# Merging two places of small work per unit into one in an encoder layer on one core

## The chip, the cores and the metric

One core of a Trainium2 chip runs the kernel. The metric is the device time of one execution in microseconds (us). TensorE (PE in the profile), VectorE (DVE), ScalarE (ACT), GpSimd (POOL) and SyncE (SP) each work through their own list in order and meet only through semaphores.

## The reference

One layer of a streaming encoder, for 512 prompt rows and 64 sample rows (576 columns once transposed), with 1024 features, in float32:

```python
h = rmsnorm(x, g_mix_pre)
q_a, k_a, v_a, q_r, k_r, v_r, g_r, gate_a, gate_r = split_in(h @ w_in)
o_a = attend(q_a, k_a, v_a, sinks)      # 8 heads, window of 128 rows, blocks of 64
o_r, ret_state = retain(rotary(q_r), rotary(k_r) * 128 ** -0.5, v_r)   # 4 heads, a state of 128 x 256
o_r = head_group_norm(o_r) * silu(g_r)
merged = sigmoid(gate_a) * (o_a @ w_branch_attn) + sigmoid(gate_r) * (o_r @ w_branch_ret)
x = x + rmsnorm(merged @ w_out, g_mix_post)
f = (silu(h2 @ w_ffn_gate) * (h2 @ w_ffn_up)) @ w_ffn_down     # h2 = rmsnorm(x, g_ffn_pre)
x = x + rmsnorm(f, g_ffn_post)
x = x + (p @ w_ple_proj) * sigmoid(x @ w_ple_gate)
```

## The kernel before

The big products are made of **units**. A unit is one 128-column tile of a weight against all 576 activation columns: 8 tiles of the contracted dimension, 3 products each (high and low parts of weight and activation), 2 halves of 288 columns, so 48 matmuls at line 683 into `acc`. Its weight is loaded by SyncE, copied to a high part by ScalarE (`split_hi`, L1140) and to a low part by VectorE (`split_lo`, L1630). When it is done VectorE takes it out of PSUM (`scaled_out`, L1660, called by `job_out` in the heads). There are two accumulators and two weight slots.

Between the matmuls of these units TensorE does the attention and the retention in small **pieces**. The layer has five rounds of six units. In round `h` = 0 to 3 the units are the projections of retention head `h` (first unit to sixth, `t` = 0 to 5); a last round is the first six of the gate units. Beside them round `h` does attention block `h` (block 4 in the last), and the retention of head `h - 1`, which takes five chunks `c`. Round 0 has no retention. Rounds 1 to 3 are one loop.

`PLACES` is a list of twelve lists of pieces, written out by hand; all engines walk the same list. The pieces are:

- `("att", "A", p)`: TensorE scores (L829), VectorE scale, mask and maximum (L1737), ScalarE exponentials (L1203).
- `("att", "N", p)`: VectorE alone: denominator, reciprocal, and four scalings of `prob` (L1749, L1751, L1754).
- `("att", "B", p)`: TensorE transposes `prob` (L838); VectorE (L1759) and ScalarE (L1209) copy them to `prob_t`. In block 0 there is only VectorE's copy.
- `("att", "C", p)`: TensorE multiplies with v (L846), ScalarE copies the result to `o_att` (L1216).
- `("ret", "A", c)`: TensorE L860 and L863, VectorE q_dec, s_dec, k_dec. `("ret", "B", c)`: TensorE L875, L877, L879; VectorE updates the state and takes the moments; GpSimd the power. `("ret", "N", c)`: VectorE norms (L1793). `("ret", "C", c)`: TensorE transposes `o_norm` (L887), VectorE multiplies with the gate (L1801).
- `("v", None, e)`: TensorE transposes half of v (L898, L899), VectorE copies it out (L1831, L1833).

TensorE, in `six_jobs`, does the even place `2t` after 24 of the 48 matmuls of unit `t`, and the odd place `2t + 1` behind its last matmul. On VectorE `head` (and the gate loop) does for each `t`: place `2t`, `job_out(t)`, place `2t + 1`, the low part of unit `t + 2`'s weight, and the rotation in `t` = 0 and 2. ScalarE does place `2t`, the high part of unit `t + 2`, its own work on unit `t` (swaps, sigmoids), place `2t + 1`. GpSimd: place `2t`, its own work, place `2t + 1`.

Waits that matter below are those on TensorE: `B` of attention waits for `att_prob` (the last scaling of `N`); `C` of attention for `att_t0` and `att_t1` (the two copies); `ret C` for `ret_norm`; `ret A` of chunk `c` for `ret_gated` of chunk `c - 2` and before; `v` for `att_out` (ScalarE's copy after `C`). On VectorE `ret C` waits for TensorE's `ret C` (`ret_C`). A place's pieces stand in order on every engine, so on VectorE place 7, `[("ret", "C", 2), ("att", "N", 1)]`, does the gate product of chunk 2 and then the scalings.

Of the kernel before, what the change touches and what calls it, by code (L numbers as in the profile page):

```python
# [14 lines left out]
P = 128  # L15
# [6 lines left out]
KD = D // P  # L22
HEADS, KV, HD = 8, 2, 64
GROUP = HEADS // KV
# [26 lines left out]
U_GATE, J_GATE = U_HEAD + 6 * RH, J_HEAD + 6 * RH  # L51
U_MRG, J_MRG = U_GATE + 8, J_GATE + 8
# [50 lines left out]
def unit(base, step=0, i=0):  # L103

    return base // 2 + (step // 2) * i, base % 2
# [6 lines left out]
def wait(eng, sem, value):  # L112

    if not (isinstance(value, int) and value <= 0):
        eng.wait_ge(sem, value)
# [4 lines left out]
    [("att", "N", 0)],  # L120
    [("ret", "B", 0), ("ret", "A", 1), ("ret", "N", 0)],
    [("att", "B", 0), ("ret", "C", 0)],
    [("att", "C", 0), ("ret", "B", 1), ("ret", "A", 2), ("ret", "N", 1)],
    [("ret", "C", 1), ("att", "A", 1)],
    [("ret", "B", 2), ("ret", "A", 3), ("ret", "N", 2)],
    [("ret", "C", 2), ("att", "N", 1)],
# [166 lines left out]
def encoder_layer(nc, x_p, x_s, p_p, p_s, cache_k, cache_v, state_in, g_mix_pre, w_in, sinks_in,  # L293
                  w_ba, w_br, w_out, g_mix_post, g_ffn_pre, w_fg, w_fu, w_fd, g_ffn_post, w_pp, w_pg,
                  table_in, scratch, y_p, y_s, k_p, v_p, r_p, k_s, v_s, r_s):
    with ExitStack() as ctx:
# [3 lines left out]
        def place(name, shape, dt=F32, at=None):  # L300

            size = int(np.prod(shape[1:])) * 4
            if at is None:
                at = cursor[0]
                cursor[0] += (size + 31) // 32 * 32
            assert at + size <= nc.sbuf_usable_end, (name, at + size, nc.sbuf_usable_end)
            return nc.alloc_sbuf_tensor_at(name, shape, dt, offset=at)
# [35 lines left out]
        xh = place("xh", [P, KD, ROWS], F32R, at=a_at)  # L343
        xl = place("xl", [P, KD, ROWS], F32R, at=b_at)
# [103 lines left out]
        att = small[:, 0:1024]  # L448
# [72 lines left out]
        def acc_of(a):  # L521
            return acc[:, a, :, 0:HALF]
# [37 lines left out]
        def halves(ap):  # L560
            return ap.rearrange("p (h n) -> p h n", h=2)
# [113 lines left out]
        def _(pe):  # L675
            def products(s, a, ks, rhs_h, rhs_l, first, last, tile_at):

                ins = None
                for n, k in enumerate(ks):
                    at = tile_at(k)  # L680
                    for m, (w, x) in enumerate(((whi, rhs_h), (whi, rhs_l), (wlo, rhs_h))):
                        for hf in range(2):
                            ins = nc.tensor.matmul(  # L683
                                acc[:, a, hf, 0:HALF], w[:, s, at:at + P], x(k)[:, hf * HALF:(hf + 1) * HALF],
                                start=first and n == 0 and m == 0, stop=last and n == len(ks) - 1 and m == 2)
                return ins

            def run_unit(vs, wa, rhs, ks=KD, k0=0, first=True, last=True, ready=None,
                         between=None):


                (v, s), (w, a) = vs, wa
                if first:
                    wait(pe, acc_free[a], w)
                pe.wait_ge(lo_ready, 2 * v + s + 1)
                rh_, rl_ = rhs
                if between is not None:
                    for part in (range(ks // 2), range(ks // 2, ks)):
                        ins = products(s, a, part, lambda k: rh_[:, k, :], lambda k: rl_[:, k, :],
                                       part[0] == 0, part[-1] == ks - 1, lambda k: k * P)  # L700
                        if part[0] == 0:
                            between()
                elif ready is None:
                    ins = products(s, a, range(ks), lambda k: rh_[:, k0 + k, :], lambda k: rl_[:, k0 + k, :],
                                   first, last, lambda k: k * P)
                else:
                    for k in range(ks):
                        ready(k0 + k)
                        ins = products(s, a, [k], lambda k: rh_[:, k0 + k, :], lambda k: rl_[:, k0 + k, :],
                                       first and k == 0, last and k == ks - 1, lambda k: k * P)  # L710
                ins.then_inc(unit_done, 1)
# [178 lines left out]
            def v_transposes(e, h):  # L890

                w, a = unit(J_HEAD + (3, 4)[e], 6, h)
                pe.wait_ge(acc_free[a], w + 1)
                wait(pe, v_rows, 2 * h + e)
                pe.wait_ge(att_t1, 2 * h + 2)
                pe.wait_ge(att_out, 2 * h + 2)
                for r in range(RT - 1):
                    nc.tensor.transpose(att[:, r * P:(r + 1) * P], zt[:, a, r * P:(r + 1) * P], ident)  # L898
                nc.tensor.transpose(att[0:DEC, SEQ:SEQ + P], zt[:, a, SEQ:ROWS], ident).then_inc(v_t, 1)  # L899

            def pieces(place, h, b, r, slot):
                for kind, piece, c in PLACES[place]:
                    if kind == "att":
                        att_piece(piece, c, b)
                    elif kind == "ret" and r is not None:
                        ret_piece(piece, c, r, slot)
                    elif kind == "v" and h is not None:
                        v_transposes(c, h)

            def six_jobs(u, j, per, i, h, b, r, slot):  # L910

                for t in range(6):
                    run_unit(unit(u + t, per, i), unit(j + t, per, i), (xh, xl),
                             between=lambda: pieces(2 * t, h, b, r, slot))
                    pieces(2 * t + 1, h, b, r, slot)

            pe.wait_ge(ckt_ready, 1)
            pe.wait_ge(kv_rows, 1)
# [702 lines left out]
        def _(dve):  # L1621
# [4 lines left out]
            def split_lo(vs, n=KD * P):  # L1626

                v, s = vs
                dve.wait_ge(hi_ready, 2 * v + s + 1)
                nc.vector.tensor_tensor(wlo[:, s, 0:n], raw[:, s, 0:n], whi[:, s, 0:n].bitcast(F32),  # L1630
                                        ALU.subtract).then_inc(lo_ready, 1)
# [25 lines left out]
            def scaled_out(dst, w, a, u):  # L1657

                dve.wait_ge(unit_done, u + 1)
                nc.vector.tensor_tensor(halves(dst), acc_of(a), halves(rb[:, :]), ALU.mult).then_inc(acc_free[a], 1)  # L1660
# [150 lines left out]
            def rotate(t, h, slot):  # L1811

                m = 2 * h + t // 2
                dve.wait_ge(swap_ready, m + 1)
                nc.vector.tensor_tensor(tb[:, :], tb[:, :], rot[:, 1, :], ALU.mult).then_inc(dve_rot, 1)
                dve.wait_ge(dve_rot, m + 1)
                dve.wait_ge(cos_ready, m + 1)
                if not isinstance(h, int):

                    dve.wait_ge(ret_A, 5 * (h - 1) + CREDIT)  # L1820
                    dve.wait_ge(ret_kst, 5 * (h - 1) + CREDIT)
                dst = (qr if t == 0 else kr)[:, span(slot, 1), 0:ROWS].rearrange("p a n -> p (a n)")
                nc.vector.tensor_tensor(dst, ta[:, :], tb[:, :], ALU.add).then_inc(rotated, 1)
# [12 lines left out]
            def pieces(place, h, b, r, slot, rslot):  # L1836
                for kind, piece, c in PLACES[place]:
                    if kind == "att":
                        att_piece(piece, c, b)
                    elif kind == "ret" and r is not None:  # L1840
                        ret_piece(piece, c, r, rslot)
                    elif kind == "v" and h is not None:
                        v_out(c, h, slot)

            def head(h, b, r, slot, rslot):
                for t in range(6):
                    pieces(2 * t, h, b, r, slot, rslot)
                    job_out(t, h)
                    pieces(2 * t + 1, h, b, r, slot, rslot)
                    split_lo(unit(U_HEAD + t + 2, 6, h))  # L1850
                    if t in (0, 2):
                        rotate(t, h, slot)

            head(0, 0, None, 0, None)
            with dve.Fori(1, RH) as h:
                head(h, h, h - 1, h % 2, (h - 1) % 2)
# [9 lines left out]
            for t in range(8):  # L1866
                if t < 6:
                    pieces(2 * t, None, RH, RH - 1, None, (RH - 1) % 2)
                w, a = unit(J_GATE + t)
                if t == 1:  # L1870
                    dve.wait_ge(g_ready, 2 * RH)
                wait(dve, gate_sig[a], t // 2)
                scaled_out(zt[:, a, :], w, a, U_GATE + t)
                if t < 6:
                    pieces(2 * t + 1, None, RH, RH - 1, None, (RH - 1) % 2)
                split_lo(unit(U_GATE + t + 2) if t < 6 else unit(U_MRG + t - 6), n=(GROUP if t == 6 else KD) * P)
                if t >= 5:
                    branch_parts(range(BRANCH_TILES[t - 5], BRANCH_TILES[t - 4]))
            def gated(u, j, per, c, n, slot, col):
# [427 lines left out]
            for n, e in enumerate(Y_ORDER):  # L2307
                _, c, h = e
# [191 lines left out]
```

## Time and profile before

| | |
|---|---|
| three runs | 986.4, 986.9, 987.0 us; median 986.9 |
| the profiled execution | 986.12 us, span 984.5 us, mean granted clock 0.999 |
| TensorE matmuls busy | 974.8 us (99% of the span) |
| VectorE, ScalarE, GpSimd busy | 634.1, 397.0, 86.5 us |
| the five rounds | from 61.7 to 319.5 us of the span |

In the profile's time tables each line is a group of instructions by source line. A matmul's listed duration runs from its start to its modelled end, and neighbours overlap, so the time that TensorE spends on something is read from one start to the next.

### The profile page before, as it was taken

What the parts mean: (1) busy time and instruction counts of PE and PEld (TensorE: products, weight loads), DVE (VectorE), ACT (ScalarE), POOL (GpSimd) and SP (SyncE); (2) the same over time, 40 slices, a digit from 0 to 9 for tenths busy, and PEclk for the clock granted to TensorE, in tenths of its full rate; (3) what the DMA queues carried; (4) which work ended last, traced back from release to release, by engine and by line L of the source; (5) the groups of instructions that cost most, each with busy time, mean ns of one, the idle gap of its engine ahead of it and who ended that gap; (6) DMA issues with size and microseconds to landing.
All of it is one profiled execution on the core that took longest, in us unless ns stands there. A gap on an engine that the chain in (4) does not pass through costs nothing.

```text
span 984.5 us, 19215 instructions
## 1 busy us (share of the span) xinstructions
PE 974.8 (99%) x7286; PEld 954.2 (97%) x7286; DVE 634.1 (64%) x1246; ACT 397.0 (40%) x695; POOL 86.5 (9%) x140
## 2 busy tenths in 40 slices
PE   9999999999999999999999999999999999999998
PEld 7999999999999999999999999999999999999997
DVE  6554676767665633445467899625996469966772
ACT  4333533434243522223555555424453234444352
POOL 2123212212100000010002000000000000030000
PEclk9999999999999999999999999999999999999999
DMA  8434222122222232245603523521334213366211
GB/s 214 137 123 121 79 66 72 46 75 62 62 70 65 76 94 78 78 129 180 179 12 122 190 79 94 150 66 44 101 108 127 73 50 107 97 202 189 86 48 50
DMA packets 166199, 98.47 MB, mean 100 GB/s; under 512 B 14657, under 2 KB 162529, under 8 KB 165873
## 3 DMA queue, kind: packets, MB, share of 16 engines
q1 hardware_dynamic: 159904, 79.19, 28.4%
q0 software_dynamic: 4336, 16.67, 4.7%
q10 hardware_dynamic: 1888, 1.64, 0.6%
q8 instruction: 48, 0.79, 0.3%
q14 instruction: 23, 0.18, 0.1%
HBM read 86.79 MB, written 10.75 MB: 99 GB/s over the span
## 4 chain that ended last, share of the span: by engine, by line
PE 91%; DVE 5%; issue 2%; ACT 1%; DMA 0%; DVEq 0%; SPq 0%; ACTq 0%
PE acc L683 34%; PE acc L960 10%; PE acc L961 10%; PE acc L962 10%; PE small L960 6%; PE small L961 6%; PE small L962 6%; PE small L829 1%; PE small L846 1%; PE small L875 1%; PE small L879 1%; PE small L877 1%; PE acc L791 1%; PE small L1114 1%; ACT prob L1203 1%
## 5 line engine op out<-in xcount | busy, mean ns | idle before, releaser
L683 PE MATMUL acc<-xh,whi 128*128 128x288 f32 x720 | 159.0, 302 | 0.7 <-DVE xl L1653 0.7
L683 PE MATMUL acc<-xl,whi 128*128 128x288 f32 x720 | 153.3, 294 | 0.0
L683 PE MATMUL acc<-xh,wlo 128*128 128x288 f32 x720 | 153.3, 294 | 0.0
L1140 ACT ACTIVATE whi<-raw 128x1024 fp32r<-128x1024 f32 (+1 forms) x61 | 61.1, 1002 | 203.7 <-PE acc L683 201.5
L683 PEld LDWEIGHTS acc<-xh,whi 128*128 128x128 f32 x720 | 113.9, 188 | 5.0 <-issue 3.4
L683 PEld LDWEIGHTS acc<-xl,whi 128*128 128x128 f32 x720 | 115.0, 188 | 0.0
L683 PEld LDWEIGHTS acc<-xh,wlo 128*128 128x128 f32 x720 | 114.9, 188 | 0.0
L1954 DVE TENSOR_TENSOR wlo<-raw,whi 128x512 fp32r<-128x512 f32 (+2 forms) x93 | 81.0, 872 | 49.9 <-ACT whi L1354 34.2
L960 PE MATMUL acc<-yh,whi 128*128 128x288 f32 x360 | 107.2, 298 | 0.6 <-DVE yl L2014 0.5
L962 PE MATMUL acc<-yh,wlo 128*128 128x288 f32 x360 | 106.1, 295 | 0.0
L1630 DVE TENSOR_TENSOR wlo<-raw,whi 128x1024 fp32r<-128x1024 f32 (+1 forms) x63 | 73.0, 1159 | 43.6 <-ACT whi L1140 43.0
L960 PE MATMUL acc<-fh,whi 128*128 128x288 f32 x264 | 77.9, 295 | 0.0
L961 PE MATMUL acc<-fl,whi 128*128 128x288 f32 x264 | 77.8, 295 | 0.0
L962 PE MATMUL acc<-fh,wlo 128*128 128x288 f32 x264 | 77.7, 294 | 0.0
L961 PE MATMUL acc<-yl,whi 128*128 128x288 f32 x264 | 77.7, 294 | 0.0
L1362 ACT ACTIVATE whi<-s_sum 128x512 fp32r<-128x512 f32 x76 | 47.7, 630 | 61.5 <-DVE s_sum L2135 50.0
L960 PEld LDWEIGHTS acc<-yh,whi 128*128 128x128 f32 x360 | 67.6, 188 | 1.1 <-DVE yl L2014 1.1
L962 PEld LDWEIGHTS acc<-yh,wlo 128*128 128x128 f32 x360 | 67.6, 188 | 0.0
L1660 DVE TENSOR_TENSOR zt<-acc,rb 128x576 f32<-128x576 f32 x40 | 30.3, 756 | 45.8 <-PE acc L683 45.8
L1954 DVE TENSOR_TENSOR wlo<-s_sum,whi 128x512 fp32r<-128x512 f32 x76 | 51.7, 684 | 8.6 <-ACT whi L1362 8.6
L1354 ACT ACTIVATE whi<-raw 128x1024 fp32r<-128x1024 f32 (+1 forms) x38 | 38.2, 1011 | 39.9 <-PE acc L962 18.1
L961 PEld LDWEIGHTS acc<-yl,whi 128*128 128x128 f32 x264 | 49.6, 188 | 0.0
(326 smaller groups left out, 2398.0 us busy)
## 6 DMA issues: line engine op xcount, KB each, us to landing
raw<-in_w_in SPq DMA_DIRECT2D x92, 256.0 KB, 3.2
raw<-in_w_ffn_gate SPq DMA_DIRECT2D x44, 256.0 KB, 3.2
raw<-in_w_ffn_up SPq DMA_DIRECT2D x44, 256.0 KB, 4.1
raw<-in_w_ffn_down SPq DMA_DIRECT2D x32, 256.0 KB, 3.6
res<-x_scratch POOLq DMA_DIRECT2D x16, 288.0 KB, 4.2
raw<-in_w_branch_ret SPq DMA_DIRECT2D x16, 256.0 KB, 3.0
raw<-in_w_out SPq DMA_DIRECT2D x16, 256.0 KB, 4.9
raw<-in_w_ffn_down SPq DMA_DIRECT2D x16, 192.0 KB, 3.7
```

The source lines that it names most:

```text
L683: ins = nc.tensor.matmul(acc[:, a, hf, 0:HALF], w[:, s, at:at + P], x(k)[:, hf * HALF:(hf + 1) * HALF], start=first and n == 0 and m == 0, ...
L791: ins = nc.tensor.matmul(acc[:, 0, hf, 0:HALF], w[:, at], x[:, k, hf * HALF:(hf + 1) * HALF], start=k == 0 and m == 0, stop=k == KD - 1 an ...
L829: ins = nc.tensor.matmul(att[0:nq, slot * KW + k0:slot * KW + k1], q_st[64 * g:64 * g + 64, 2 * p + j, 0:nq], k_st[64 * g:64 * g + 64, k0: ...
L960: nc.tensor.matmul(bank, w_h, x_h, start=first, stop=False)
L961: nc.tensor.matmul(bank, w_h, x_l, start=False, stop=False)
L962: return nc.tensor.matmul(bank, w_l, x_h, start=False, stop=last)
L1140: nc.scalar.activation(whi[:, s, 0:n], raw[:, s, 0:n], ACT.Copy).then_inc(hi_ready, 1)
L1354: nc.scalar.activation(dst[:, 0:n], raw_of(RAW[u])[:, 0:n], ACT.Copy).then_inc(hi_ready, 1)
L1362: nc.scalar.activation(dst[:, 0:QUART], s_sum[:, S_STEP[u[2]], :], ACT.Copy).then_inc(hi_ready, 1)
L1630: nc.vector.tensor_tensor(wlo[:, s, 0:n], raw[:, s, 0:n], whi[:, s, 0:n].bitcast(F32), ALU.subtract).then_inc(lo_ready, 1)
L1660: nc.vector.tensor_tensor(halves(dst), acc_of(a), halves(rb[:, :]), ALU.mult).then_inc(acc_free[a], 1)
L1954: nc.vector.tensor_tensor(dst[:, 0:n], src[:, 0:n], high[:, 0:n], ALU.subtract).then_inc(lo_ready, 1)
```

## The change

Two edits of order on TensorE, one on VectorE, and one list reordered. TensorE does both the odd place `2t - 1` and the even place `2t` in the middle of unit `t`, one right behind the other; place 11 stays behind unit 5. On VectorE the odd place is moved behind the low part and the rotation. Place 4 is reordered so that `("att", "C", 0)` is its last piece. ScalarE and GpSimd keep their order, except for place 4, where each of them has at most one of its kinds in the same order as before.

```diff
@@ PLACES
     [("att", "B", 0), ("ret", "C", 0)],
-    [("att", "C", 0), ("ret", "B", 1), ("ret", "A", 2), ("ret", "N", 1)],
+    [("ret", "B", 1), ("ret", "A", 2), ("ret", "N", 1), ("att", "C", 0)],
     [("ret", "C", 1), ("att", "A", 1)],
@@ TensorE, six_jobs
+                def inside(t):
+                    if t > 0:
+                        pieces(2 * t - 1, h, b, r, slot)
+                    pieces(2 * t, h, b, r, slot)
+
                 for t in range(6):
-                    run_unit(unit(u + t, per, i), unit(j + t, per, i), (xh, xl),
-                             between=lambda: pieces(2 * t, h, b, r, slot))
-                    pieces(2 * t + 1, h, b, r, slot)
+                    run_unit(unit(u + t, per, i), unit(j + t, per, i), (xh, xl), between=lambda: inside(t))
+                pieces(11, h, b, r, slot)
@@ VectorE, head
                     job_out(t, h)
-                    pieces(2 * t + 1, h, b, r, slot, rslot)
                     split_lo(unit(U_HEAD + t + 2, 6, h))
                     if t in (0, 2):
                         rotate(t, h, slot)
+                    pieces(2 * t + 1, h, b, r, slot, rslot)
@@ VectorE, gate units
                 scaled_out(zt[:, a, :], w, a, U_GATE + t)
+                split_lo(unit(U_GATE + t + 2) if t < 6 else unit(U_MRG + t - 6), n=(GROUP if t == 6 else KD) * P)
                 if t < 6:
                     pieces(2 * t + 1, None, RH, RH - 1, None, (RH - 1) % 2)
-                split_lo(unit(U_GATE + t + 2) if t < 6 else unit(U_MRG + t - 6), n=(GROUP if t == 6 else KD) * P)
```

## Rows read from the trace of the kernel before

**Rows 1.** The page: busy us, share of the span and instructions of each engine.
```profile
PE 974.8 (99%) x7286; PEld 954.2 (97%) x7286; DVE 634.1 (64%) x1246; ACT 397.0 (40%) x695; POOL 86.5 (9%) x140
```

**Rows 2.** Stretches: round 2, last round (length, busy us by engine, clock, DMA).
```profile
160.16:215.28 55.12, 54.94 (x401) 51.41 (x401) 38.36 (x99) 21.66 (x39) 11.07 (x18) 1.00 0.22 64
...
270.35:319.45 49.10, 49.10 (x368) 46.03 (x368) 29.43 (x89) 18.18 (x37) 4.58 (x10) 1.00 0.23 68
```

**Rows 3.** Waits of TensorE, 60 to 330 us: total us, times, longest.
```profile
PE small L887 <- DVE o_norm L1793: 0.6, 3, 0.2
```

**Rows 4.** Timeline of TensorE, round 2, end of unit 3, middle of 4: start, us.
```profile
192.50 0.38 PE L887 MATMUL small<-tab,o_norm 128*128 128x128 f32 x2
192.63 0.51 PE L683 MATMUL acc<-xh,whi 128*128 128x288 f32 x2
192.98 0.42 PE L683 MATMUL acc<-xl,whi 128*128 128x288 f32 x2
...
195.89 1.03 PE L838 MATMUL small<-tab,prob 128*128 128x128 f32 x8
196.76 0.60 PE L875 MATMUL small<-vr,s_dec 128*128 x2
```

**Rows 5.** The chain of waits in order of time, round 2: start, us, what.
```profile
178.21 0.63 PE small L875 x2
...
192.88 3.17 PE acc L683 x24
...
196.92 0.43 PE small L875 x2
...
202.96 3.37 PE acc L683 x24
```

**Rows 6.** Timeline of TensorE and VectorE, round 2, end of unit 1.
```profile
172.30 1.03 PE L838 MATMUL small<-tab,prob 128*128 128x128 f32 x8
173.52 0.44 PE L887 MATMUL small<-tab,o_norm 128*128 128x128 f32 x2 [0.18 <-DVE o_norm L1793]
...
172.91 0.54 DVE L1793 TENSOR_SCALAR o_norm<-small,moments,grstd 128x256 f32<-128x256 f32 x1
```

**Rows 7.** Timeline of VectorE, round 2, place 7 and the copy of place 8.
```profile
193.37 0.41 DVE L1801 TENSOR_TENSOR o_ret<-small,gr 128x256 f32 x1
193.70 0.15 DVE L1749 TENSOR_TENSOR den<-den,sink_exp 128x4 f32<-128x4 f32 x1
...
194.10 1.14 DVE L1754 TENSOR_SCALAR prob<-prob,den 128x256 f32<-128x256 f32 x4
...
196.96 0.69 DVE L1759 COPY prob_t<-small 128x512 f32<-128x512 f32 x1 [0.58 <-PE small L838]
```

**Rows 8.** Timeline of VectorE, last round, place 7.
```profile
302.23 0.41 DVE L1801 TENSOR_TENSOR o_ret<-small,gr 128x256 f32<-128x256 f32 x1
...
302.95 1.00 DVE L1754 TENSOR_SCALAR prob<-prob,den 64x192 f32<-64x192 f32 x4
```

**Rows 9.** Timeline of ScalarE, VectorE and TensorE, round 0, units 3 and 4.
```profile
86.94 1.06 ACT L1140 ACTIVATE whi<-raw 128x1024 fp32r<-128x1024 f32 x1 [1.65 <-PE acc L683]
...
88.02 0.88 DVE L1754 TENSOR_SCALAR prob<-prob,den 128x128 f32<-128x128 f32 x4
88.81 1.22 DVE L1630 TENSOR_TENSOR wlo<-raw,whi 128x1024 fp32r<-128x1024 f32 x1
90.49 0.69 DVE L1759 COPY prob_t<-small 128x512 f32<-128x512 f32 x1 [0.46 <-PE small L838]
...
89.85 0.60 PE L838 MATMUL small<-tab,prob 128*128 128x128 f32 x4
```

**Rows 10.** Timeline of TensorE and ScalarE, round 2: attention C and its copy.
```profile
201.88 1.08 PE L846 MATMUL small<-prob_t,v_st 128*64 128x256 f32 x8
...
203.17 0.39 ACT L1216 ACTIVATE o_att<-small 128x256 f32 x1 [0.35 <-PE small L846]
```

**Rows 11.** Stretch at the end of the span: last column but two is the clock.
```profile
982.00:984.50 2.50, 0.00 (x0) 0.00 (x0) 0.00 (x0) 0.00 (x0) 0.00 (x0) 0.61 0.23 59
```

## The prediction

> **What bounds the kernel now.** I read the page first: TensorE is busy 974.8 of 984.5 us, the next engine 634.1 [rows 1]. So a change of order can save only what TensorE waits or loses at a switch, and a new wait on TensorE is paid in full, because no idle time behind it can take it up. Then the stretches: round 2 takes 55.12 us and the last round 49.10, with the clock at 1.00 and VectorE busy 38.36 of 55.12 [rows 2]. Rounds 1 and 3 repeat round 2 within 0.05 us. Then TensorE's waits: in all five rounds there is one kind, `ret C` for `o_norm`, three times [rows 3]. The timelines give the sizes of the rest.
>
> **What a stop of the unit's stream costs.** The change moves 19 groups of pieces on TensorE from a unit's end to a middle: places 3, 5, 7 and 9 in four rounds, and 3, 5 and 9 in round 0, where place 7 has nothing for TensorE (nor has place 1 anywhere). 18 of them join a stop that exists already. In steady stream 24 matmuls take 3.17 us, 0.264 a pair [rows 5]. At the end of unit 3 `ret C` starts at 192.50 and the next unit's first pair at 192.63; that pair takes 0.35 instead of 0.264, so the stop takes 0.13 + 0.09 = 0.22 us. Eight transposes take 196.76 - 195.89 = 0.87, 0.109 each, so the two of `ret C` are 0.22 by themselves [rows 4]. A stop costs nothing beyond its own work, and merging stops gains 0 to 0.02 each; I take 0. The pieces on half the rows (attention A and C) lose about 0.2 us behind them, into the main stream (3.37 against 3.17) as into another piece (0.63 against 0.43 for the same pair) [rows 5]. Place 4's reordering therefore exchanges one such loss for an equal one: 0, at most 0.1 a round either way.
>
> **What is saved.** At the end of unit 1 the transposes of attention B start at 172.30 and need 0.87, but `ret C` starts at 173.52, behind `o_norm`, which VectorE ends at 173.45 [rows 6]. 173.52 - 173.17 = 0.35 us, and 0.3 to 0.4 in rounds 1 and 3 (three waits [rows 3]): 1.1 us. With the change `ret C 0` comes 3.2 us later and this wait goes. VectorE's low parts now stand earlier, but TensorE waits for none of them today, so that is worth 0.
>
> **What is added.** The same rule for each: two pieces that were half a unit (3.2 us of TensorE's own work) apart are now neighbours, and where another engine has a step between them TensorE stands.
>
> *Place 7 to place 8, rounds 1 to 3.* TensorE does `ret C 2`, then attention B 1, which needs the scalings of N 1. VectorE has N 1 behind its own `ret C 2`, and that waits for TensorE's `ret C 2`, now in the middle of unit 4. So the whole VectorE chain starts only then. From a transposition's listed end to VectorE's start takes 0.04 us (195.89 + 1.03 = 196.92, start 196.96) [rows 4, 7]; `ret C` is listed at 0.38 [rows 4], so VectorE starts at +0.42. From its `ret C` to the end of the last scaling it is 194.10 + 1.14 - 193.37 = 1.87 [rows 7], and back to TensorE 0.07 (173.45 to 173.52 [rows 6]): +2.36. Without the wait TensorE would go on at +0.22. **2.14 us a round, 6.4 in three.** Behind the waiting VectorE instruction stand only the copy of B 1 and `ret B 3`, for which TensorE isn't yet ready.
>
> *The same in the last round.* 302.95 + 1.00 - 302.23 = 1.72 [rows 8] in place of 1.87: **2.0 us.**
>
> *Round 0.* It has no `ret C`, but N 1 moves behind the low part of unit 5, whose high part ScalarE ends at 88.00 [rows 9]. Low part 1.15 (its 1.22 less the overlap with its successor), 0.40 to the scalings [rows 7], 0.88 for them [rows 9] and 0.1 of hand-over: 90.53, where B 1 starts at 89.85 today [rows 9]. **0.7 us.** Also, with no retention between them B 0 and C 0 are now neighbours: B starts, VectorE's copy starts 0.64 later (90.49 against 89.85) and takes 0.69 [rows 9], +1.39 with the hand-over, against 0.54 for four transposes and the switch: **0.85 us.** And C 1 and `v 0`: ScalarE starts 0.21 after C's listed end (201.88 + 1.08 to 203.17) and takes 0.39 [rows 10]; C of block 0 has half the passes, some 0.65 listed, so +1.3 against 0.55: **0.75 us.**
>
> *What is covered.* In rounds 1 to 4 `ret B 1` and `ret A 2` (1.3 + 0.33) stand between B 0 and C 0. VectorE's copy and `ret C 0` are done at 1.07 + 0.6 + 0.4 = 2.1 us after B's start, `ret A 2` comes at 0.87 + 0.22 + 1.3 = 2.4, C 0 at 2.8. `ret B 4` (1.3) stands between C 1 and `v 0`, and ScalarE needs 0.7. For place 5 `ret C 1`, VectorE comes from the rotation some 0.9 us late, but `ret A 3`, which wants its result, comes 2.7 us later. Bounds: 0 if the covers hold, 0.3 to 0.5 a piece in four rounds if one is short, 2 us. I take 0. VectorE's bunched work (3 to 5 us behind each middle) fits the 3.2 us of the second half and the pieces before it, with 0.2 to 0.8 us left in units 3 and 5; what is late first is `job_out`, which has a whole unit of slack. The branch parts behind the last round start about a low part (1.2 us [rows 9]) later, and their first reader comes two units (4 x 3.17 us) behind.
>
> **The sum.** 6.4 + 2.0 + 0.7 + 0.85 + 0.75 - 1.1 = 9.6 us. On the profiled execution: 986.1 + 9.6 = 995.7 us. The median of the runs is 0.8 above it, which gives 996.5; between them **996**. Bounds of the terms: each chain of place 7 can be 0.3 shorter or 0.2 longer, round 0's three together 1.0 to 2.8: 994 to 998.5.
>
> **The clock, against the trace.** The granted clock is 1.00 in every round, and the one stretch below it is the last 2.5 us, 0.61, when TensorE had run dry [rows 11]; the change adds four holes of 2 us in the middle of a unit. The Trainium skill ("TensorE: Matmul & The Clock Gate", section "HAM oscillation — how this bites in real kernels") says that waits between bursts of matmuls can throttle the array and that every burst after them then starts cold. If each of the four holes cost the 3.17 us half behind it at 1.2 GHz, twice as long, it would be 4 x 3.2 = 13 us on top. The end of the span agrees in direction; no row shows a 2 us hole inside a busy stretch.
>
> **Rivals.**
> *A. The stops are what costs, and the time falls.* Were the switch between float32 pieces and the stream expensive, 19 groups merged would each return it. For it: a round's 55.12 less twelve halves of 3.17 leaves 17.1, of which the passes explain 15.1, so 1.9 is lost at borders. Against: 4 x 0.3 to 0.4 of that stands at the half-row pieces, which keep their borders, and 0.35 is `o_norm`. It decides from (9.6 / 19) 0.5 us a stop; at 0.55 each: 986.1 + 9.6 - 10.5 = 985.2 us.
> *B. The chain of place 7 is mostly covered.* If VectorE could take N 1 ahead (TensorE and the exponentials were early enough) only round 0 and a hand-over of 0.5 us a round stay: 2.3 + 2 - 1.1 = 3.2, 989.5 us. Against: one list, one order, and VectorE executes in order.
> *C. A cover is short.* VectorE's bunched work makes TensorE wait at C 0, `ret A` or `v` too, 1 to 1.5 us a round in four rounds: 5 on top, 1001.
> *D. The clock falls* behind the new holes: 1009.
>
> **How the numbers follow.** Forecast 72%, C 10%, B 9%, A 5%, D 4%. The range from 991 to 1001 leaves out A, B's lower half, D and half of C; the forecast's own is 994 to 998.5. No change can be told within 0.2% (2 us). Slower by more: forecast, C, D and B (3.2 us, its lower part within 2): 0.92. Same: 0.04; faster: 0.04, both from A.
>
> **What would show it.** Round 2 at 55.1 + 2.14 - 0.35 = 56.9 us, the last at 51.1, and round 0 longer by 2.3. A new row in TensorE's waits, L838 for VectorE's `prob` (L1754), five times and about 2 us in four of them; no `ret C` wait for `o_norm`; in round 0 waits of L846 for `prob_t` and of L898 for `o_att`. After the rounds nothing changes: the stretch from the rounds' end to the span's end stays at 665 us. Wrong would be: no L838 wait, halves shorter than 3.17, a clock below 1.00 in the rounds, or waits for the low part at L683.

## The result: 1003.4 us, slower by 1.6%

| | before | after |
|---|---|---|
| median of 5 runs each | 986.7 us | 1003.4 us (1000.1 to 1003.6) |
| ratio | 1 | 1.0163 (95%: 1.0150 to 1.0175) |
| profiled execution: span, granted clock | 984.5 us, 0.999 | 1001.7 us, 0.995 |
| round 0, from first to next attention A | 43.30 us | 46.34 us |
| rounds 1, 2, 3 | 55.13, 55.12, 55.07 | 59.19, 59.03, 57.31 |
| last round, to the first unbroken unit behind it | 49.10 | 52.62 |
| from there to the end of the span | 665.05 | 665.08 |

The direction was forecast, the size was not: 996 us with a range to 1001. The five rounds together are 16.8 us longer, the rest is equal within 0.1, but for 0.4 us while the input loads. That part ahead of the rounds takes 61.7 to 63.7 us in the profiled executions of this document, though no edit touches it; so a difference of 1 to 2 us between two medians says less than the stretches of the rounds. The stretches of the changed kernel, columns as in [rows 2]:

```profile
108.47:167.66 59.19, 56.82 (x402) 52.53 (x401) 39.37 (x99) 22.04 (x39) 11.76 (x19) 0.97 0.22 66
167.66:226.69 59.03, 56.89 (x402) 52.62 (x401) 39.26 (x99) 21.83 (x39) 11.02 (x18) 0.97 0.21 60
226.69:284.00 57.31, 55.16 (x402) 51.22 (x403) 39.26 (x99) 21.84 (x41) 11.01 (x18) 1.00 0.21 62
```

The third column from the end answers to the 1.00 of [rows 2]: it is 0.97 in rounds 1 and 2 and 1.00 in round 3. Where it is 1.00 the round is 1.7 to 1.9 us shorter. TensorE's waits, which before had one kind in the rounds [rows 3]:

```profile
PE small L838 <- DVE prob L1758: 9.4, 5, 2.1
...
PE small L846 <- DVE prob_t L1763: 0.9, 1, 0.9
PE small L898 <- ACT o_att L1220: 0.7, 1, 0.7
```

These are the three handovers of the prediction, and `o_norm` is gone. Their sum is 11.0 us and the rounds grew by 16.8. The timeline of TensorE in round 2, the middle of unit 4 (before: [rows 4]), shows what the list of waits doesn't:

```profile
203.04 0.38 PE L887 MATMUL small<-tab,o_norm 128*128 128x128 f32 x2
205.56 1.78 PE L838 MATMUL small<-tab,prob 128*128 128x128 f32 x8 [2.13 <-DVE prob L1758]
207.13 1.06 PE L875 MATMUL small<-vr,s_dec 128*128 x2
207.99 1.06 PE L877 MATMUL small<-state_p,q_dec 128*128 128x256 f32 x2
208.84 0.78 PE L879 MATMUL small<-vr,k_dec 128*128 x2
209.46 0.38 PE L860 MATMUL small<-qr,rk_st 128*128 x2
```

From 203.04 to 205.56 there is 0.22 us of work and 2.30 of idle. Then eight transposes take 1.57 us (205.56 to 207.13) where they took 0.87 in [rows 4], and L875, L877 and L879 take 0.86, 0.85 and 0.62 in place of 0.43 each, until with L860 the normal pace is back. Together 1.7 us. From B 1 to attention C 1 it takes 10.90 us here (205.56 to 216.46) and 9.22 in round 3; I call such a stretch at the low clock a **dip**, and the idle time before it a **hole**. The same place in round 3, where nothing is slow:

```profile
262.02 0.38 PE L887 MATMUL small<-tab,o_norm 128*128 128x128 f32 x2
264.54 1.09 PE L838 MATMUL small<-tab,prob 128*128 128x128 f32 x8 [2.14 <-DVE prob L1758]
265.47 0.60 PE L875 MATMUL small<-vr,s_dec 128*128 x2
```

The stretches behind the holes of rounds 2, 1 and 3, and of the last round:

```profile
205.56:209.50 3.94, 3.94 (x15) 3.50 (x16) 0.69 (x1) 0.60 (x1) 0.00 (x0) 0.57 0.04 12
146.56:150.50 3.94, 3.94 (x18) 3.45 (x19) 1.17 (x3) 0.60 (x1) 0.00 (x0) 0.65 0.03 9
264.50:268.50 4.00, 3.96 (x28) 3.81 (x29) 2.03 (x7) 0.60 (x1) 0.10 (x1) 1.00 0.05 16
320.30:324.30 4.00, 3.98 (x21) 3.57 (x22) 1.50 (x6) 0.39 (x1) 0.00 (x0) 0.69 0.14 42
```

The granted clock is 0.57, 0.65, 1.00 and 0.69 there. So in three of the four retention rounds the clock fell from 2.4 to 1.2 GHz behind an idle hole, for the larger part of these stretches, and in round 3 it did not behind an equal hole. It did not fall in the hole itself: when TensorE had begun again, the clock was still at 2.4 GHz for 1.21 us in round 1, 0.24 in round 2 and 1.53 in the last. Executions of the one kernel differ: four of the five runs took 1003.3 to 1003.6 us at clock 0.994 or 0.995, the fifth 1000.1 us at 0.997, so it seems to have had fewer dips (only one run has a trace).

| the 16.8 us by part | forecast | measured in the profiled rounds |
|---|---|---|
| idle at place 7 to 8, rounds 1 to 3 and last | 6.4 + 2.0 | 3 x 2.30 + 1.98 = 8.9 |
| the same in round 0 (N 1 behind the low part) | 0.7 | 92.58 - 91.20 = 1.4 |
| round 0, B 0 to C 0 and C 1 to v 0 | 0.85 + 0.75 | 0.94 + 0.76 = 1.7 |
| slow passes behind three holes (B 1 to C 1, with the dip less without) | 0 | 10.87 and 10.90 less 9.22, last round 10.61 less 9.01 (experiments 1 and 2): 4.9 |
| wait for o_norm gone | -1.1 | -1.1 |
| rest, 0.5 in round 1, 0.3 in rounds 2 and 3 (retention A 2 late by 0.4 and 0.17, borders) | 0 | 1.0 |
| sum | 9.6 | 16.8 |

### The profile page after: what moved, and what is told of

Its sections match the earlier page's. It is cut to its first block, busy times and chain, and to the rows that moved or that the text cites. A ratio compares the mean times of both kernels' runs of the same rounds, so it can differ in the third digit from the quotient of the medians.

```text
span 1001.7 us, 19215 instructions
## 1 busy us (share of the span) xinstructions
PE 980.1 (98%) x7286; PEld 957.1 (96%) x7286; DVE 638.8 (64%) x1246; ACT 398.0 (40%) x695; POOL 85.4 (9%) x140
## 4 chain that ended last, share of the span: by engine, by line
PE 92%; DVE 4%; issue 1%; ACT 1%; DMA 1%; SPq 0%; DVEq 0%; ACTq 0%
PE acc L683 35%; PE acc L964 10%; PE acc L966 10%; PE acc L965 10%; PE small L964 6%; PE small L965 6%; PE small L966 6%; PE small L875 1%; PE small L879 1%; PE small L838 1%; PE small L846 1%; PE small L829 1%; PE small L877 1%; PE acc L791 1%; PE small L860 1%
## 5 line engine op out<-in xcount | busy, mean ns | idle before, releaser
L1634 DVE TENSOR_TENSOR wlo<-raw,whi 128x1024 fp32r<-128x1024 f32 (+1 forms) x63 | 79.3, 1259 | 55.4 <-ACT whi L1144 54.9
```

## The experiments

"Before" below is the kernel before, run on the same chip in the same turns (three groups of runs, each on a chip of its own); its medians were 986.5 to 986.9 us.

**1. Place 7 turned round.** All engines do N 1 ahead of C 2:

```diff
-    [("ret", "C", 2), ("att", "N", 1)],
+    [("att", "N", 1), ("ret", "C", 2)],
```

> The changed kernel with place 7 turned round: attention N 1 ahead of retention C 2, on every engine. VectorE can then scale prob before TensorE reaches C 2. Theory (a hole of 2.3 us in each of four rounds, and behind three of them a stretch at 1.2 GHz that costs 1.75 us): both go, 4 x 2.3 + 3 x 1.75 = 14.4 us less than 1003.4, so 989 us, granted clock 1.00 in all rounds, round 0 still 3.0 us longer than before the change. Rival (bunching the small work is itself what costs, VectorE is late all over): the time falls by less than half of that, to 996 or more. Rival (the clock falls for the new order of pieces, not for the hole): 994, with the clock still 0.97 in three rounds.

Measured 992.8 us, 1.0059 of before (1.0045 to 1.0073). Both the holes of 2.3 us and the slow passes are gone, 10.6 us. The theory wanted 14.4; a smaller hole is left. TensorE in round 2:

```profile
200.69 0.38 PE L887 MATMUL small<-tab,o_norm 128*128 128x128 f32 x2
201.61 1.09 PE L838 MATMUL small<-tab,prob 128*128 128x128 f32 x8 [0.54 <-DVE prob L1758]
```

201.61 - 200.69 - 0.22 = 0.70 us idle: VectorE does N 1 behind the low part of unit 5 (1.14 us, and 0.22 of waiting for ScalarE's high part before it), and it comes to it late, behind a low part of unit 4 that took 2.25 us in place of 1.22 (more on that behind experiment 10). No slow passes follow. Neither rival fits: the clock is 1.00 in all rounds.

**2. The hole filled with useless matmuls.**

```diff
+                    if t == 4 and r is not None:
+                        for _ in range(10):
+                            nc.tensor.matmul(ret_dl[:, 0:P], ones[:, :], ones[:, :], start=True, stop=True)
```

> The changed kernel with ten float32 matmuls of ones by ones (128x128x128, about 2.2 us at full clock) between places 7 and 8 in the rounds with retention; their result is used by nothing. TensorE now works in the hole but is not earlier at attention B 1. Theory (the idle hole makes the granted clock fall): the hole's 2.3 us stay, the slow passes behind it go: 1003.4 - 5.2 = 998 us, clock 1.00 in the rounds. Rival (the passes behind the hole are slow because of the bunched pieces or of contention on PSUM, and the clock column only reports it): still 1003 to 1004, attention B's eight transposes still 1.6 us.

Measured 999.6 us, 1.0126 (1.0111 to 1.0142); 998 was expected. TensorE in round 2, and the stretch of that round:

```profile
202.49 0.38 PE L887 MATMUL small<-tab,o_norm 128*128 128x128 f32 x2
202.70 2.40 PE L917 MATMUL small<-ones 128*128 128x128 f32 x20
205.00 1.09 PE L838 MATMUL small<-tab,prob 128*128 128x128 f32 x8
205.93 0.60 PE L875 MATMUL small<-vr,s_dec 128*128 x2
```

```profile
167.13:224.46 57.33, 57.32 (x421) 53.50 (x421) 39.24 (x99) 21.82 (x39) 11.00 (x18) 1.00 0.21 62
```

Attention B starts as late as with the hole (2.3 us behind C 2), and its eight transposes take 0.93 again. 57.33 us is round 3 of the changed kernel (57.31), which had the hole and no dip. So the hole's own length and the slow passes are two costs, and the second hangs on TensorE being idle. The five rounds take 270.0 us, 4.5 less than in the changed kernel. Useless work made the kernel faster. (The profiled execution has one low clock some 12 us into the span, ahead of the rounds; the rounds have none.)

**3. Retention in the hole.**

```diff
-    [("att", "B", 1), ("ret", "B", 3), ("ret", "A", 4), ("ret", "N", 3)],
+    [("ret", "B", 3), ("ret", "A", 4), ("ret", "N", 3), ("att", "B", 1)],
```

> The changed kernel with place 8 reordered: retention B 3, A 4, N 3 ahead of attention B 1 (as the change itself did in place 4). Retention B 3 and A 4 take 1.3 + 0.33 us of TensorE and need only VectorE's gate product, so they fill 1.6 us of the 2.3 us hole. Theory: a hole of 0.65 us stays, too short to move the clock: 1003.4 - 4 x 1.6 - 5.2 = 992 us, clock 1.00. Rival (any stop for VectorE in the middle drops the clock): 997, clock still 0.97 in three rounds. Rival (bunching costs): over 997.

Measured 993.0 us, 1.0057 (1.0043 to 1.0071), as expected within 1. Round 2:

```profile
201.15 0.60 PE L875 MATMUL small<-vr,s_dec 128*128 x2
...
202.70 0.27 PE L863 MATMUL small<-tab,rk_st 128*128 128x128 f32 x1
203.45 1.09 PE L838 MATMUL small<-tab,prob 128*128 128x128 f32 x8 [0.48 <-DVE prob L1758]
```

From 202.81 to 203.45, 0.64 us, TensorE is idle, and no pass behind is slow: the clock is 1.00 in all rounds.

**4. VectorE's order back**, the odd place ahead of the low part and the rotation, here and in the same way in the gate units; TensorE as changed:

```diff
                     job_out(t, h)
+                    pieces(2 * t + 1, h, b, r, slot, rslot)
                     split_lo(unit(U_HEAD + t + 2, 6, h))
                     if t in (0, 2):
                         rotate(t, h, slot)
-                    pieces(2 * t + 1, h, b, r, slot, rslot)
```

> The changed kernel with VectorE's order as before the change (the odd place ahead of the low part and the rotation), TensorE and place 4 as changed. Theory (round 0's longest new wait, 1.4 us at attention B 1, comes from N 1 standing behind the low part): round 0 gets 1.4 us shorter, the four holes at place 7 stay as they are, since there VectorE waits for TensorE's retention C 2 in either order: 1002 us. The low parts then come after the holes, some 3.6 us before they are needed, so they add nothing. Rival (the low parts' place decides, and late ones stop the stream): waits of L683 for the low part, 1006 or more.

Measured 1001.9 us, 1.0142 (1.0124 to 1.0160): as expected. The wait of L838 in round 0 is gone (8.2 us in four, where it was 9.4 in five), the four of 2 us are there. One of its five runs took 997.6 us at clock 0.999, the others 1001.6 to 1002.4 at 0.992 to 0.995. The profiled one (1001.9) has three dips, and 1001.9 less three dips of 1.6 to 1.7 us is 997: it looks like the same kernel with and without them.

**5. One edit to the kernel before: retention C 0 later.**

```diff
-    [("att", "B", 0), ("ret", "C", 0)],
-    [("att", "C", 0), ("ret", "B", 1), ("ret", "A", 2), ("ret", "N", 1)],
+    [("att", "B", 0)],
+    [("ret", "C", 0), ("att", "C", 0), ("ret", "B", 1), ("ret", "A", 2), ("ret", "N", 1)],
```

> The kernel before the change, with one edit: retention C 0 moved from the end of unit 1 (place 3) to the head of place 4 in the middle of unit 2. Theory: this takes the wait for o_norm (0.35 us in three rounds) and nothing else; 986.9 - 1.1 = 985.8 us, no L887 wait left. Rival (the wait only moves, VectorE being late from round to round): 986.9 as before.

Measured 985.6 us, 0.9988 (0.9979 to 0.9997): the only kernel here that beats the one before, by 0.1%. The view of TensorE's waits has no row left in the rounds. Round 2 (55.12 before [rows 2]):

```profile
160.29:214.94 54.65, 54.65 (x401) 51.39 (x401) 38.45 (x99) 21.67 (x39) 10.98 (x18) 1.00 0.22 65
```

**6. Place 7 turned round and VectorE's order back** (edits 1 and 4).

> The changed kernel with place 7 turned round and VectorE's odd places ahead of the low parts again; TensorE still does both places in the middle. In the run with place 7 alone turned round, TensorE still stood 0.7 us before attention B 1 in each round and 1.4 in round 0. Theory (that rest is N 1 standing behind the low part, which waits for ScalarE's high part): it goes, 992.8 - 4 x 0.7 - 1.4 = 988.6 us. What is left over before the change is round 0's B-C and C-v waits (1.5 us) and 0.2 us a round at retention A 2, less the 1.1 saved. Rival (VectorE is simply late there, with its bunched work): 992 to 993.

Measured 993.5 us, 1.0064 (1.0050 to 1.0078): a miss, the theory's 988.6 is out. Round 0's wait went (44.9 us against 46.3) and so did the hole of the last round, but the hole of rounds 1 to 3 grew from 0.70 to 1.48. VectorE in round 2:

```profile
191.59 0.42 DVE L1805 TENSOR_TENSOR o_ret<-small,gr 128x256 f32 x1 [2.80 <-PE small L887]
...
194.72 1.23 DVE L1634 TENSOR_TENSOR wlo<-raw,whi 128x1024 fp32r<-128x1024 f32 x1
195.86 0.75 DVE L1819 TENSOR_TENSOR tb<-tb,rot 128x576 f32<-128x576 f32 x1
...
199.90 0.75 DVE L1664 TENSOR_TENSOR zt<-acc,rb 128x576 f32<-128x576 f32 x1
...
200.97 1.14 DVE L1758 TENSOR_SCALAR prob<-prob,den 128x256 f32<-128x256 f32 x4
```

VectorE idles 2.80 us for TensorE's C 1, and then has attention A 1, the low part, the rotation and retention B 2, A 3 and N 2 in one piece up to 200. The unit's result waits for it (0.75 at 199.90), and N 1 behind that ends at 202.1, where TensorE wanted it at 200.7. So the rival's reason is right here (its 992 to 993 is just missed): with this order VectorE is late. Between experiments 1 and 6 the change's order of VectorE is thus worth 0.5 to 0.7 us in each of rounds 1 to 3 and costs 1.4 in round 0 and 0.4 in the last: nearly nothing in sum. The three holes of 1.5 us brought no dip: clock 1.00 in the rounds.

**7. Round 0 apart**: the kernel of 6 with TensorE's round 0 as before the change (`if r is None` the old loop of `six_jobs`).

> The kernel of z1 with round 0's places apart on TensorE as before the change (the odd place at the unit's end); rounds 1 to 4 merged. Theory (in round 0 no retention stands between B 0 and C 0 or between C 1 and v 0, so merging costs 0.76 + 0.7 us there): 1.5 us less than z1, 987.1 us, equal to the kernel before within 0.5 us, so merging as such neither gains nor costs. Rival (merging stops saves switching, 0.05 us or more a stop): 985.9 or less. Rival (bunching costs): 988.5 or more.

Measured 991.0 us, 1.0044 (1.0031 to 1.0058). The step of 2.5 us from 6 is larger than the 1.5 expected; in the profiled executions round 0 gives 1.6 (43.30 us, exactly before's, against 44.89), and the part ahead of the rounds is 1.3 shorter, where nothing was changed. The level is off for the same reason as in 6.

**8. Place 4 in its old order** (attention C 0 first, otherwise as changed).

> The changed kernel with place 4 in its old order, attention C 0 first. Theory (C 0 then follows B 0 with only retention C 0 between, and VectorE's copy ends 1.83 us after B's start where TensorE comes at 1.09): a wait of 0.75 us at L846 in each of rounds 1 to 4, and retention A 2's 0.2 us wait goes: 1003.4 + 4 x 0.55 = 1005.6 us; should the clock fall for more of the holes, up to 1.75 us on top. Rival (the reordering is what brought the slow passes): 1000 or less.

Measured 1004.5 us, 1.0172 (1.0156 to 1.0188). The expected 1005.6 is missed by 1.1. The waits are there, 0.66 us in each of rounds 1 to 3 and 0.24 in the last (3.1 in all, with round 0's 0.9), where 0.75 was expected in four:

```profile
PE small L846 <- DVE prob_t L1763: 3.1, 5, 0.9
```

In the profiled execution the clock fell in two rounds instead of three, which hides part of it; round 3, with no dip in either, is 57.76 against 57.31. The reordering of place 4 is worth some 0.45 us in each of rounds 1 to 3 to the changed kernel.

**9. The chain alone in the kernel before.** Nothing merged, VectorE's order as before:

```diff
-    [("ret", "C", 2), ("att", "N", 1)],
-    [("att", "B", 1), ("ret", "B", 3), ("ret", "A", 4), ("ret", "N", 3)],
+    [],
+    [("ret", "C", 2), ("att", "N", 1), ("att", "B", 1), ("ret", "B", 3), ("ret", "A", 4), ("ret", "N", 3)],
```

> The kernel before the change, with one edit of PLACES: place 7 emptied and its two pieces put ahead of attention B 1 in place 8, so that retention C 2, N 1 and B 1 follow each other in the middle of unit 4 as in the changed kernel. No place is merged, VectorE's order is as before. Theory: this handover alone makes the idle stretch of 2.3 us in rounds 1 to 3 and 2.1 in the last, 0.7 us in round 0, and up to four dips of the clock behind them at 1.75 us: 986.9 + 9.0 + 0.7 + 3.5 to 7 = 1000 to 1003.6 us, with slow passes behind attention B 1. Rival (it needs the merged places or VectorE's changed order as well): 992 or less.

Measured 999.1 us, 1.0131 (1.0116 to 1.0147), 0.9 below the expected band. One handover makes 12.6 of the change's 16.7 us; in the profiled rounds it is 11.2 of 16.8. Round 2 and the last:

```profile
164.41:221.83 57.42, 55.10 (x401) 51.37 (x401) 38.52 (x99) 21.71 (x39) 11.11 (x18) 1.00 0.21 62
...
279.25:331.82 52.57, 50.76 (x368) 47.55 (x368) 29.58 (x89) 18.23 (x37) 4.59 (x10) 0.97 0.22 63
```

Rounds 1 to 3 are longer by 2.3 each with the clock at 1.00, the last by 3.5 with it at 0.97: here one hole of four brought a dip. The runs go from 998.4 us (clock 0.997) to 1000.9 (0.994).

**10. Merged and covered**: edits 1, 3 and 7, VectorE's order as changed.

> The changed kernel with all three remedies: place 7 turned round (N 1 first), place 8 with retention B 3 and A 4 ahead of attention B 1, round 0 apart on TensorE; VectorE's order as changed. Theory (only handovers without cover cost): rounds 1 to 4 like before the change less 0.35 for o_norm in three, plus 0.2 each at retention A 2; round 0 keeps 0.7 us at B 1 with N 1 behind the low part: 986.9 - 1.1 + 0.8 + 0.7 = 987.3 us, clock 1.00. Rival (merging stops pays once covered): 985.5 or less. Rival (VectorE bunched is late anyway): 990 or more.

Measured 988.8 us, 1.0021 (1.0012 to 1.0030), where 987.3 was expected; neither rival. Rounds 1 to 3 take 55.51, 55.22 and 55.19 us, the last 49.12, no more than 0.4 over before's; round 0 keeps 1.45 at attention B 1 instead of 0.7. Together that is 2.1 us. The only waits in the rounds:

```profile
PE small L838 <- DVE prob L1764: 1.2, 1, 1.2
...
PE small L860 <- issue: 0.3, 1, 0.3
```

**A side effect that the traces of all the kernels show.** In the change's order VectorE does the low part of unit 4's weight right behind the result of unit 2, and so beside GpSimd's multiplication `ta`, which starts with the same result; the low part of unit 2 stands behind unit 0 in the same way. Round 0 of the changed kernel, and the same low part before:

```profile
82.20 2.19 DVE L1634 TENSOR_TENSOR wlo<-raw,whi 128x1024 fp32r<-128x1024 f32 x1 [0.40 <-ACT whi L1144]
...
81.89 1.42 POOL L2398 TENSOR_TENSOR ta<-zt,rot 128x576 f32<-128x576 f32 x1 [4.13 <-DVE zt L1664]
```

```profile
82.10 1.22 DVE L1630 TENSOR_TENSOR wlo<-raw,whi 128x1024 fp32r<-128x1024 f32 x1
```

Each of the six kernels with the change's order of VectorE has eight such low parts, of units 2 and 4 in rounds 0 to 3: 1.66 to 1.68 us where 0.6 us of them lie beside `ta`, 2.08 to 2.26 where 1.0 to 1.2 do. The six with the old order (experiments 4 to 7 and 9, and the kernel before) have none beside `ta`, and one of 1.57 us in experiments 4 and 6, 0.5 us of it beside another such multiplication (`gr`). A low part at 533.38 us of the changed kernel, wholly beside GpSimd's power of 96 x 3 elements, takes 1.22.

## Why the prediction was wrong

**What bounds the kernel, and that waits on TensorE are paid in full:** right. Behind the rounds the two traces agree within 0.1 us.

**A stop costs nothing by itself:** right. 16 stops fewer in experiment 10 made no round shorter, though the 0.35 us of `o_norm` is gone in three; experiment 5 gets that gain with no merging. A gain of a few hundredths a stop could hide behind retention A 2's delay, but not rival A's 0.5.

**Place 7 to 8:** the place, the mechanism and the count are right, and 2.30 stands for 2.14. The missing 0.16 is VectorE's start, 0.58 us behind `ret C`'s start (203.04 to 203.62) where I had taken 0.42 from a wait behind other transposes; the chain itself took 1.88 against 1.87.

**"The clock falls", rival D at 4%:** this is the step that failed. The sum priced a hole at its length alone, and gave the clock only the form of all or nothing (13 us on top). In three of four rounds the clock fell, and each fall cost 1.6 to 1.7 us: 4.9 of the 7.2 us that the forecast was short. Experiment 2 shows it: the same delay with TensorE busy, and the passes are fast. Experiments 3, 4 and 9 agree. The page of the Trainium skill that the prediction cited ("TensorE: Matmul & The Clock Gate", section "HAM oscillation — how this bites in real kernels") warned rightly that waits between bursts can throttle. That every burst behind them starts cold the traces do not bear out: round 3 stayed at 2.4 GHz, and in the others the clock fell only when TensorE had begun again. The measured price was less than half of what I had built on it, since the clock did not fall behind every hole, and where it did, it was low for less work than the half unit that I had taken: in round 2 for the small pieces, in round 1 and the last for some of these and the first matmuls of the half unit. I had weighed it by the trace of before, in which [rows 11] shows the low clock only when TensorE had run dry, and that trace has no idle of this size inside the rounds; it could not speak against the rule.

**Round 0, N 1:** 1.4 instead of 0.7 us. I had let ScalarE begin unit 5's high part at the unit's end, as in [rows 9]. In the changed kernel it began 0.7 us behind the unit's end (88.3), after the exponentials of A 1:

```profile
82.20 2.19 DVE L1634 TENSOR_TENSOR wlo<-raw,whi 128x1024 fp32r<-128x1024 f32 x1 [0.40 <-ACT whi L1144]
84.31 0.75 DVE L1819 TENSOR_TENSOR tb<-tb,rot 128x576 f32<-128x576 f32 x1
...
88.93 0.19 ACT L1209 ACTIVATE sink_exp<-top 128x4 f32<-128x4 f32 x1
89.03 1.04 ACT L1144 ACTIVATE whi<-raw 128x1024 fp32r<-128x1024 f32 x1
```

Attention A 1 came half a unit later and the low part ahead of it on VectorE took 2.19 us instead of 1.22, beside GpSimd's `ta` (81.89 to 83.31). At 1.22 the exponentials would have ended before the unit did, an estimate from these rows. So a queue that I had called ready was not, because its work comes from the pieces that had moved. That the 1.4 us is N 1 behind the low part is shown by experiment 4. In all twelve traces a low part takes 1.5 us or more only beside a GpSimd multiplication; no run took the multiplication away.

**The covers:** they held at C 0 and at `v 0` of the later rounds. At `ret A 2` I had 0.3 us in hand, but it starts 0.17 late (185.54 against 185.37) in rounds 2 and 3, and 0.4 late in round 1, where VectorE's product also waited for GpSimd's `gr`:

```profile
184.67 0.42 DVE L1805 TENSOR_TENSOR o_ret<-small,gr 128x256 f32 x1
...
185.54 0.48 PE L860 MATMUL small<-qr,rk_st 128*128 x2
```

VectorE's product ends 2.1 us behind B's start (182.98 to 185.09), as estimated. What I had wrong is the way back: TensorE starts 0.45 behind it, in round 1 too, and not 0.07 as at `ret C`; why is open. With the half-row borders this is the 0.3 to 0.5 us a round that I had priced at 0.

**VectorE's room:** with the change's own order it fitted, as said. With the old order it does not once place 7 is turned round (experiment 6), which I had not expected.

**Open:** what decides whether a hole of 2.0 to 2.3 us brings a dip. Of the sixteen such holes in the profiled executions nine did: three of four in the changed kernel and in experiment 4, two in experiment 8, one in experiment 9; and runs of one kernel differ. Holes of 1.5 us and less (experiments 1, 3, 6, 7 and 10, and round 0 everywhere) brought none.

## What to carry to other kernels

When two groups of small work are moved together, list for each engine what the second needs from the first: a pair that passes through another engine needs that engine's whole chain as idle time, and order inside the merged list (independent work between, the other engine's long step first) decides more than the number of stops. Price an idle hole of TensorE at its length and a possible dip of the clock behind it; if it can't be closed, useless matmuls in it were better than none here. And follow a moved piece into the queues that it feeds: what was ready in the old trace may be late in the new one.

## What the runs showed of the hardware that I had not expected

- A hole of 2.0 to 2.3 us in a TensorE that is otherwise 99% busy was enough to bring the granted clock from 2.4 to 1.2 GHz (0.57 mean over the 3.94 us behind it), in nine of sixteen cases. It fell only when TensorE had begun again (0.24 to 1.53 us later in the changed kernel). The pair of L875 then takes 0.86 us instead of 0.43, and one such dip costs 1.6 to 1.7 us.
- Ten useless matmuls in each of four such holes made the kernel 3.8 us faster (1003.4 to 999.6), though they kept the holes' length.
- VectorE's low part of 1.22 us (one 128 x 1024 tile less another) took 2.08 to 2.26 us beside 1.0 to 1.2 us of a GpSimd multiplication of 128 x 576, and 1.66 to 1.68 beside 0.6 us of it, in all six kernels where the two met; beside a GpSimd power of 96 x 3 it took 1.22.
